# Two chained model blocks on one core: the order of VectorE's scalings and low halves in the norm between the blocks, and the PSUM banks around it

## The chip, the cores and the metric

The kernel runs on 1 core of one Trainium2 chip. The metric is the device time of one execution in microseconds (us), median of several. An engine is named as follows: TensorE (PE in the profile, PEld its weight loads), VectorE (DVE), ScalarE (ACT), GpSimd (POOL), SyncE (SP). All instruction streams run in order on their engine; semaphores tie them together.

## The reference

Two transformer blocks of different kind work on x, 512 tokens by 1024 channels in float32. The first mixes pooled averages and three-branch sparse attention and has a squared-ReLU feed-forward part; it ends with a norm. The second has a forgetting attention and a stick-breaking attention, 8 heads each, and 16 experts, of which each token takes 2. Where the one hands over to the other stands this:

```python
    x = x + jnp.square(jax.nn.relu(h @ w_ff1[l])) @ w_ff2[l]
    return rms_norm(x, norm_final)                      # end of the first block
...
    h = rmsnorm(x, norm1_g[l]) * (1.0 + scale1) + shift1    # start of the second
    proj = h @ w_in[l]
    qa, ka, va, fa, qb, kb, vb, ga, gb = jnp.split(proj, IN_SPLITS_2, axis=-1)
    log_f = jax.nn.log_sigmoid((fa + b_forget[l]).astype(jnp.float32)).transpose(0, 2, 1)
```

scale1 and shift1 come from a small product of the input c with ada_w. So the change stands between two norms in a row: that of norm_final, whose result is x from there on, and that of norm1_g.

## The kernel before, in words

All activations are held transposed: channels on the 128 partitions, the 512 tokens along the free axis, so x is eight row blocks X[:, k, :] of 128 by 512. A dense product is made in float32 precision from three passes in the fast format: each operand is split into a high half (ScalarE, a copy that rounds) and a low half (the difference). For weights the high half is L286 on ScalarE and the low half L291, in this part of the program on GpSimd. A weight tile of 128 by 1024 is loaded by SyncE's queue into one of five raw buffers and split into one of four split buffers. A written plan (make_plan) lists all weight tiles in order of use, and for each tile which later tile is loaded and which is split in its turn. `dense` (L417, L418, L421) is 24 matmuls of 128 by 512 for one output block; `dense_two` (L439, L440, L443) makes two output blocks at once and goes through the eight input blocks k in the outer loop, so that it can start when block 0 of the input is there: six matmuls for each k.

PSUM has eight banks. `Psum.take` gives the next matmul group a bank from a set, in turn: each set has its own counter. If the bank's last holder has not been read out, TensorE waits for the eviction before the group's first matmul. RB is the set of banks 0 to 6, ALL8 all eight. Bank 7 is otherwise kept for attention outputs and for the modulation's sums.

The norm between the blocks goes like this. ScalarE squares the row blocks, plain and times norm_final, VectorE and GpSimd add the squares up, and TensorE sums each over the partitions: `row_sums`, keys ("rms", 3) and ("rms", 4). ScalarE and VectorE make the two factors for each token from these, `diagonal` puts them into a diagonal matrix, and `spread` has TensorE spread them over the partitions: ("rmsb", 3) is the factor of norm_final, ("rmsb", 4) that of both norms together. Then for each row block k

- VectorE scales: TMP[k % 4] = X[k] * gsc * ps["rmsb", 4] (L1910),
- ScalarE adds shift1 and rounds: RH[0, k] (L1207),
- VectorE makes the low half: RH[1, k] = TMP + shift1 - RH[0, k] (L1913),

and TensorE, which waits for the low half of k, takes this block into dense_two with the tiles ("w2_fa", 0), the forget gates, and ("w2_qa", 0), the first of four for the queries. Behind the loop VectorE applies norm_final to the eight blocks of X in place (L1916).

The VectorE loop as it was, with the three instructions in this order for each k:

```python
            dve.scalar_tensor_tensor(TMP[:, j, :], X[:, k, :], gsc[:, 16 + k:17 + k], ps["rmsb", 4], ALU.mult,
...
            dve.wait_ge(*A(("h2", k)))
            dve.scalar_tensor_tensor(RH[:, 1, k, :], TMP[:, j, :], modt[:, k:k + 1], hif(RH[:, 0, k, :]), ALU.add,
```

What each engine has next. TensorE: dense products for ("w2_qa", 1), ("w2_qa", 2), ("w2_qa", 3), ("w2_ka", 0), ("w2_ka", 1) and then the first attention scores (`pair_scores(0)`, L753 and L758). ScalarE: the high half of a weight tile, ("w2_qa", 2); then the log-sigmoid chain for the forget gates, which starts by evicting ("w2_fa", 0) at L984 and goes on with an absolute value, exponential and logarithm (L1251 to L1255, with two loads of activation tables); then the high half of ("w2_qa", 3), and only then the eviction of ("w2_qa", 0) into PC, at L984 too, which stands in the same helper; then the high half of ("w2_ka", 0), the eviction of ("w2_qa", 1), and so on in turn. GpSimd: low halves of the same tiles. VectorE: the updates of X, then its part of the chain, which ends in a running sum along the tokens. SyncE: stores that sum to HBM, loads it back as rows spread over all partitions (L2551, four rows of 256 KB at first), which VectorE adds to the first scores (L1934), and loads the coming weight tiles.

Later follow the second attention's remaining parts, the output product, a third norm with the router, and the expert stage: for each unit of 128 token rows twelve weight tiles are loaded (w_gate, w_up, w_down), split by ScalarE (L286) and VectorE (L291), and used by TensorE.

Of the kernel before, what the change touches and what calls it, by code (L numbers as in the profile page):

```python
# [12 lines left out]
ALU = mybir.AluOpType  # L13
# [89 lines left out]
def hif(ap):  # L103
    return ap.bitcast(F32)
# [54 lines left out]
def build_program(nc, t, ctx):  # L159
    def sb(name, shape, dt=F32):  # L160
        return ctx.enter_context(nc.sbuf_tensor(name, shape, dt))

    def mark(name, step=1):
        m = Mark(ctx.enter_context(nc.semaphore(name)), step)
        marks.append(m)
        return m
# [3 lines left out]
    RH = sb("RH", [128, 2, 8, S], F32R)  # L170
# [4 lines left out]
    X = sb("X", [128, 8, S])  # L175
# [6 lines left out]
    TMP = sb("TMP", [128, 4, S])  # L182
# [10 lines left out]
    modt = sb("modt", [128, 48])  # L193
    gsc = sb("gsc", [128, 32])
# [9 lines left out]
    ps = Psum([ctx.enter_context(nc.psum_tensor(f"ps{i}", [128, 512], F32))[:, :] for i in range(8)])  # L204
# [4 lines left out]
    A = mark("act_done")  # L209
    LOV = mark("dve_weights_lo")  # L210
    V = mark("dve_done")
# [30 lines left out]
    for n, (name, u, kind) in enumerate(plan):  # L242
# [3 lines left out]
        if kind == "split":  # L246
            k = len(spl)
# [26 lines left out]
    def lo(n):  # L274

        return LOV(n) if lo_by[n] == "dve" else LOP(n)
# [31 lines left out]
    RST, GTS = RT[:, 0:512], RT[:, 512:704]  # L308
    NR = small[:, 32:56]
    SQ2 = PB[:, 0, 0:512]  # L310
# [45 lines left out]
    RB = (0, 1, 2, 3, 4, 5, 6)  # L356
# [37 lines left out]
    def tensor(pe):  # L394
        ps.restart()

        def take(key, banks=ALL8):
            b = ps.take(key, banks)
            if ps.prev[key] is not None:
                pe.wait_ge(*freed(ps.prev[key]))  # L400
            return b
# [25 lines left out]
        def dense_two(units, R, ready, banks=ALL8):  # L427

            tiles_ = [IDX[u] for u in units]
            bs = [take(u, banks) for u in units]  # L430
            for k in range(8):
                pe.wait_ge(*ready(k))
                for key, n, b in zip(units, tiles_, bs):
                    s, c = spl[n], 128 * k
                    wh, wl = RS[:, s, 0, c:c + 128], RS[:, s, 1, c:c + 128]
                    xh, xl = R[:, 0, k, :], R[:, 1, k, :]
                    if k == 0:
                        pe.wait_ge(*HI(n))
                    pe.matmul(b[:, :], wh, xh, start=(k == 0), stop=False)  # L439
                    pe.matmul(b[:, :], wh, xl, start=False, stop=False)  # L440
                    if k == 0:
                        pe.wait_ge(*lo(n))
                    last = pe.matmul(b[:, :], wl, xh, start=False, stop=(k == 7))  # L443
                    if k == 7:
                        last.then_inc(*P.up(key, ("fed", n)))
# [30 lines left out]
        def row_sums(key, acc, banks=ALL8):  # L476
            b = take(key, banks)
            for i in range(4):
                last = pe.matmul(b[:, i:i + 1], acc[:, 128 * i:128 * i + 128], onesf[:, 0:1], start=True, stop=True)
            last.then_inc(*P.up(key))  # L480

        def spread(key, j, banks=ALL8):
            b = take(key, banks)
            pe.wait_ge(*V(("dg", key)))
            pe.matmul(b[:, :], onesf[:, :], TMP[:, j, :], start=True, stop=True).then_inc(*P.up(key))
# [247 lines left out]


        pe.wait_ge(*V(("sq3", 7)))
        row_sums(("rms", 3), RST)
        pe.wait_ge(*V(("sq4", 7)))
        row_sums(("rms", 4), SQ2)
        spread(("rmsb", 4), 3, (4,))
        spread(("rmsb", 3), 2, (5,))  # L740


        def pair_scores(n):
# [49 lines left out]
        def projected(name, *us):  # L793
            for u in us:
                dense(name, u, RH, 0, 8, None, RB)

        dense_two([("w2_fa", 0), ("w2_qa", 0)], RH, lambda k: V(("h2", k)), (0, 1))
        projected("w2_qa", 1, 2, 3)
        projected("w2_ka", 0, 1)
        pair_scores(0)  # L800
# [651 lines left out]
    def vector(dve):  # L1452
        def tt(out, a, b, op, *keys):
            dve.tensor_tensor(out, a, b, op).then_inc(*V.up(*keys))  # L1454

        def after(*keys):

            for k in keys:
                dve.wait_ge(*V(k))
# [5 lines left out]
        def diagonal(key, col, j):  # L1465

            dg = TMP[:, j, :].rearrange("p (i n) -> p i n", i=4)
            tt(dg, identf[:, :].unsqueeze(1).broadcast_to([128, 4, 128]),
               NR[:, col:col + 4].unsqueeze(2).broadcast_to([128, 4, 128]), ALU.mult, ("dg", key))
# [223 lines left out]
        for n in range(18):  # L1693
# [14 lines left out]
            if n >= 3 and n % 2 == 1:  # L1708
                k = n // 2 - 1
# [188 lines left out]
        after("n2c")  # L1898
        diagonal(("rmsb", 4), 4, 3)
        diagonal(("rmsb", 3), 0, 2)  # L1900
        for k in range(8):
            j = k % 4
            if k == 0:
                dve.wait_ge(*P(("rmsb", 4)))
                after("ggs")
            elif k == 2:
                dve.wait_ge(*P(("rmsb", 3)))
            elif k >= 4:
                dve.wait_ge(*A(("h2", k - 4)))
            dve.scalar_tensor_tensor(TMP[:, j, :], X[:, k, :], gsc[:, 16 + k:17 + k], ps["rmsb", 4], ALU.mult,  # L1910
                                     ALU.mult).then_inc(*V.up(("h2w", k), ("ev", ("rmsb", 4))))
            dve.wait_ge(*A(("h2", k)))
            dve.scalar_tensor_tensor(RH[:, 1, k, :], TMP[:, j, :], modt[:, k:k + 1], hif(RH[:, 0, k, :]), ALU.add,  # L1913
                                     ALU.subtract).then_inc(*V.up(("h2", k)))
        for k in range(8):
            dve.scalar_tensor_tensor(X[:, k, :], X[:, k, :], GM_VECS(VG_FIN, k), ps["rmsb", 3], ALU.mult,  # L1916
                                     ALU.mult).then_inc(*V.up(("x2", k), ("ev", ("rmsb", 3))))
# [569 lines left out]
    def sync(sp):  # L2487
# [109 lines left out]
        sp.wait_ge(*OUT("all"))  # L2597

    engines = ((tensor, "tensor"), (scalar, "scalar"), (vector, "vector"), (gpsimd, "gpsimd"), (sync, "sync"))
    for body, _ in engines:  # L2600
        body(Dry())
    for m in marks:
        m.counting, m.n = False, 0
    block = ctx.enter_context(nc.Block())
    block.sync(sync)
    block.tensor(tensor)
    block.scalar(scalar)
    block.vector(vector)
    block.gpsimd(gpsimd)

# [140 lines left out]
```

## Time and profile before

| | |
|---|---|
| median of 3 runs | 1658.87 us (1653.78 to 1660.69) |
| the profiled execution | 1657.32 us |
| its span | 1655.5 us |
| TensorE busy | 1544.0 us, 93% of the span |
| VectorE busy | 894.5 us, 54% |
| ScalarE busy | 742.1 us, 45% |
| GpSimd busy | 679.8 us, 41% |
| mean granted TensorE clock | 0.976 of full speed |

The span is the time from the first to the last instruction of the profiled execution; its own time includes what lies around it. Busy time of TensorE counts overlapping matmuls once; where TensorE is the bound, only its idle time and stretches at a lower clock can be won. [...] A start-to-start distance in the timeline says how fast instructions follow each other; the duration of one can be longer, as they overlap.

### The profile page before, as it was taken

What the parts mean: (1) busy time and instruction counts of PE and PEld (TensorE: products, weight loads), DVE (VectorE), ACT (ScalarE), POOL (GpSimd) and SP (SyncE); (2) the same over time, 40 slices, a digit from 0 to 9 for tenths busy, and PEclk for the clock granted to TensorE, in tenths of its full rate; (3) what the DMA queues carried; (4) which work ended last, traced back from release to release, by engine and by line L of the source; (5) the groups of instructions that cost most, each with busy time, mean ns of one, the idle gap of its engine ahead of it and who ended that gap; (6) DMA issues with size and microseconds to landing.
All of it is one profiled execution on the core that took longest, in us unless ns stands there. A gap on an engine that the chain in (4) does not pass through costs nothing.

```text
span 1655.5 us, 19634 instructions
## 1 busy us (share of the span) xinstructions
PE 1544.0 (93%) x7371; PEld 1205.5 (73%) x7371; DVE 894.5 (54%) x1448; ACT 742.1 (45%) x1187; POOL 679.8 (41%) x421
## 2 busy tenths in 40 slices
PE   7988899999999999999986999999998899999982
PEld 6664566888887888888874777768886777777762
DVE  5357886143144665748325232441024689999984
ACT  5225786223243223232343544532233477777762
POOL 3244566444574646464552644735563200000003
PEclk9998999999999999999998999999998999999996
DMA  6420000422236584856321421112343799999944
GB/s 243 141 86 14 1 1 14 147 89 94 97 115 216 211 294 182 295 188 231 114 77 35 144 78 64 64 52 89 102 168 130 281 348 385 385 382 383 386 168 167
DMA packets 78542, 275.66 MB, mean 167 GB/s; under 512 B 9508, under 2 KB 10836, under 8 KB 78440
## 3 DMA queue, kind: packets, MB, share of 16 engines
q1 hardware_dynamic: 69712, 245.89, 41.6%
q10 hardware_dynamic: 6424, 20.05, 3.1%
q0 software_dynamic: 2304, 8.39, 1.4%
q8 instruction: 61, 1.00, 0.3%
q14 instruction: 41, 0.34, 0.1%
HBM read 243.84 MB, written 30.45 MB: 166 GB/s over the span
## 4 chain that ended last, share of the span: by engine, by line
PE 76%; DVE 10%; ACT 5%; issue 3%; POOL 2%; DMA 1%; PEldq 0%; SPq 0%; ACTq 0%; DVEq 0%; POOLq 0%
PE ps L417 16%; PE ps L421 16%; PE ps L418 16%; PE ps L922 2%; ACT RS L286 2%; PE ps L918 2%; PE ps L919 2%; PE ps L439 2%; DVE RS L291 2%; PE ps L443 2%; PE ps L440 2%; POOL RS L291 1%; PE ps L945 1%; PE ps L949 1%; PE ps L630 1%
## 5 line engine op out<-in xcount | busy, mean ns | idle before, releaser
L291 POOL TENSOR_TENSOR RS<-RAW,RS 128x1024 fp32r<-128x1024 f32 x174 | 433.2, 2492 | 448.8 <-ACT RS L286 448.6
L286 ACT ACTIVATE RS<-RAW 128x1024 fp32r<-128x1024 f32 x306 | 318.2, 1054 | 257.3 <-PE ps L421 147.4
L417 PE MATMUL ps<-RH,RS 128*128 128x512 f32 x816 | 325.3, 399 | 16.2 <-ACT RS L286 8.4
L421 PE MATMUL ps<-RH,RS 128*128 128x512 f32 x816 | 320.4, 393 | 1.2 <-POOL RS L291 1.2
L418 PE MATMUL ps<-RH,RS 128*128 128x512 f32 x816 | 320.3, 392 | 0.0
L417 PEld LDWEIGHTS ps<-RH,RS 128*128 128x128 f32 x816 | 154.8, 190 | 52.0 <-ACT RS L286 16.8
L421 PEld LDWEIGHTS ps<-RH,RS 128*128 128x128 f32 x816 | 154.7, 190 | 35.4 <-POOL RS L291 2.0
L418 PEld LDWEIGHTS ps<-RH,RS 128*128 128x128 f32 x816 | 154.9, 190 | 33.1 <-issue 1.4
L291 DVE TENSOR_TENSOR RS<-RAW,RS 128x1024 fp32r<-128x1024 f32 x132 | 154.8, 1220 | 24.1 <-ACT RS L286 23.6
L417 PE MATMUL ps<-RA,RS 128*128 128x512 f32 x400 | 157.5, 394 | 0.0
L418 PE MATMUL ps<-RA,RS 128*128 128x512 f32 x400 | 156.2, 390 | 0.0
L421 PE MATMUL ps<-RA,RS 128*128 128x512 f32 x400 | 156.1, 390 | 0.0
L2478 POOL DMA_INDIRECT PC<-ys,POS x2 | 1.9, 968 | 320.0 <-PEq L388 319.7
L922 PE MATMUL ps<-RS,RH 128*128 128x512 f32 x256 | 101.4, 396 | 7.4 <-DVE RS L291 7.4
L918 PE MATMUL ps<-RS,RH 128*128 128x512 f32 x256 | 102.7, 401 | 4.6 <-ACT RS L286 4.6
L1454 DVE TENSOR_TENSOR TMP<-TMP,ps 128x512 f32<-128x512 f32 x48 | 32.7, 685 | 128.1 <-ACT TMP L1172 72.4
L919 PE MATMUL ps<-RS,RH 128*128 128x512 f32 x256 | 99.8, 390 | 0.0
L417 PEld LDWEIGHTS ps<-RA,RS 128*128 128x128 f32 x400 | 75.4, 188 | 18.5 <-issue 3.0
L418 PEld LDWEIGHTS ps<-RA,RS 128*128 128x128 f32 x400 | 75.5, 189 | 15.9 <-issue 0.4
L421 PEld LDWEIGHTS ps<-RA,RS 128*128 128x128 f32 x400 | 75.4, 189 | 15.8
L1454 DVE TENSOR_TENSOR TMP<-ps,RT 128x512 f32<-128x512 f32 (+1 forms) x43 | 29.4, 686 | 73.1 <-PE ps L421 50.0
L922 PEld LDWEIGHTS ps<-RS,RH 128*128 128x128 f32 x256 | 48.0, 188 | 23.2 <-DVE RS L291 13.5
(357 smaller groups left out, 2633.6 us busy)
## 6 DMA issues: line engine op xcount, KB each, us to landing
RAW<-in_w_ff SPq DMA_DIRECT2D x64, 512.0 KB, 5.1
RAW<-in_w_gate SPq DMA_DIRECT2D x46, 512.0 KB, 6.3
RAW<-in_w_up SPq DMA_DIRECT2D x45, 512.0 KB, 7.2
RAW<-in_w_down SPq DMA_DIRECT2D x39, 512.0 KB, 6.0
PB<-in_ada SPq DMA_DIRECT2D x24, 512.0 KB, 4.3
TB<-in_ada SPq DMA_DIRECT2D x24, 512.0 KB, 4.4
xs<-TB SPq DMA_DIRECT2D x23, 512.0 KB, 8.6
M<-in_w_down SPq DMA_DIRECT2D x17, 512.0 KB, 6.0
```

The source lines that it names most:

```text
L286: act.activation(RS[:, spl[n], 0, :], raws[slot[n]], ACT.Copy).then_inc(*HI.up(n))
L291: eng.tensor_tensor(RS[:, s, 1, :], raws[slot[n]], hif(RS[:, s, 0, :]), ALU.subtract).then_inc(*mark.up(n))
L417: pe.matmul(b[:, :], wh, xh, start=(k == 0), stop=False)
L418: pe.matmul(b[:, :], wh, xl, start=False, stop=False)
L421: last = pe.matmul(b[:, :], wl, xh, start=False, stop=(k == K - 1))
L439: pe.matmul(b[:, :], wh, xh, start=(k == 0), stop=False)
L440: pe.matmul(b[:, :], wh, xl, start=False, stop=False)
L443: last = pe.matmul(b[:, :], wl, xh, start=False, stop=(k == 7))
L918: pe.matmul(b[:, :], xh, wh, start=(k == 0), stop=False)
L919: pe.matmul(b[:, :], xlo, wh, start=False, stop=False)
L922: last = pe.matmul(b[:, :], xh, wl, start=False, stop=(k == 7))
L1454: dve.tensor_tensor(out, a, b, op).then_inc(*V.up(*keys))
```

## The change

On VectorE, the scaling of block k + 1 is put ahead of the low half of block k. The scaling into TMP slot k % 4 waits for the low half of block k - 4 instead of for ScalarE's copy of it. On TensorE, the two sums of squares, the factor ("rmsb", 4) and the two tiles of dense_two take their banks in turn from RB; the factor ("rmsb", 3) goes to bank 7.

```diff
--- before.py
+++ after.py
@@ -733,11 +733,11 @@
 
 
         pe.wait_ge(*V(("sq3", 7)))
-        row_sums(("rms", 3), RST)
+        row_sums(("rms", 3), RST, RB)
         pe.wait_ge(*V(("sq4", 7)))
-        row_sums(("rms", 4), SQ2)
-        spread(("rmsb", 4), 3, (4,))
-        spread(("rmsb", 3), 2, (5,))
+        row_sums(("rms", 4), SQ2, RB)
+        spread(("rmsb", 4), 3, RB)
+        spread(("rmsb", 3), 2, (7,))
 
 
         def pair_scores(n):
@@ -794,7 +794,7 @@
             for u in us:
                 dense(name, u, RH, 0, 8, None, RB)
 
-        dense_two([("w2_fa", 0), ("w2_qa", 0)], RH, lambda k: V(("h2", k)), (0, 1))
+        dense_two([("w2_fa", 0), ("w2_qa", 0)], RH, lambda k: V(("h2", k)), RB)
         projected("w2_qa", 1, 2, 3)
         projected("w2_ka", 0, 1)
         pair_scores(0)
@@ -1898,20 +1898,24 @@
         after("n2c")
         diagonal(("rmsb", 4), 4, 3)
         diagonal(("rmsb", 3), 0, 2)
+        def h2_lo(k):
+            dve.wait_ge(*A(("h2", k)))
+            dve.scalar_tensor_tensor(RH[:, 1, k, :], TMP[:, k % 4, :], modt[:, k:k + 1], hif(RH[:, 0, k, :]), ALU.add,
+                                     ALU.subtract).then_inc(*V.up(("h2", k)))
+
         for k in range(8):
-            j = k % 4
             if k == 0:
                 dve.wait_ge(*P(("rmsb", 4)))
                 after("ggs")
             elif k == 2:
                 dve.wait_ge(*P(("rmsb", 3)))
             elif k >= 4:
-                dve.wait_ge(*A(("h2", k - 4)))
-            dve.scalar_tensor_tensor(TMP[:, j, :], X[:, k, :], gsc[:, 16 + k:17 + k], ps["rmsb", 4], ALU.mult,
+                after(("h2", k - 4))
+            dve.scalar_tensor_tensor(TMP[:, k % 4, :], X[:, k, :], gsc[:, 16 + k:17 + k], ps["rmsb", 4], ALU.mult,
                                      ALU.mult).then_inc(*V.up(("h2w", k), ("ev", ("rmsb", 4))))
-            dve.wait_ge(*A(("h2", k)))
-            dve.scalar_tensor_tensor(RH[:, 1, k, :], TMP[:, j, :], modt[:, k:k + 1], hif(RH[:, 0, k, :]), ALU.add,
-                                     ALU.subtract).then_inc(*V.up(("h2", k)))
+            if k >= 1:
+                h2_lo(k - 1)
+        h2_lo(7)
         for k in range(8):
             dve.scalar_tensor_tensor(X[:, k, :], X[:, k, :], GM_VECS(VG_FIN, k), ps["rmsb", 3], ALU.mult,
                                      ALU.mult).then_inc(*V.up(("x2", k), ("ev", ("rmsb", 3))))
```

How it moves instructions, first on VectorE. These are its first rows from the loop, before and after (L1910 became L1914, L1913 became L1903); the rows ahead of them are the same in both.

Before:

```order
733 L1910 SCALAR_TENSOR_TENSOR TMP<-X,gsc,ps 128x512 [waits dve_done,pe_done]
734 L1913 SCALAR_TENSOR_TENSOR RH<-TMP,modt,RH 128x512 [waits act_done]
735 L1910 SCALAR_TENSOR_TENSOR TMP<-X,gsc,ps 128x512
736 L1913 SCALAR_TENSOR_TENSOR RH<-TMP,modt,RH 128x512 [waits act_done]
737 L1910 SCALAR_TENSOR_TENSOR TMP<-X,gsc,ps 128x512 [waits pe_done]
738 L1913 SCALAR_TENSOR_TENSOR RH<-TMP,modt,RH 128x512 [waits act_done]
739 L1910 SCALAR_TENSOR_TENSOR TMP<-X,gsc,ps 128x512
740 L1913 SCALAR_TENSOR_TENSOR RH<-TMP,modt,RH 128x512 [waits act_done]
741 L1910 SCALAR_TENSOR_TENSOR TMP<-X,gsc,ps 128x512 [waits act_done]
742 L1913 SCALAR_TENSOR_TENSOR RH<-TMP,modt,RH 128x512 [waits act_done]
```

Here each scaling is followed by its own low half. After:

```order
733 L1914 SCALAR_TENSOR_TENSOR TMP<-X,gsc,ps 128x512 [waits dve_done,pe_done]
734 L1914 SCALAR_TENSOR_TENSOR TMP<-X,gsc,ps 128x512
735 L1903 SCALAR_TENSOR_TENSOR RH<-TMP,modt,RH 128x512 [waits act_done]
736 L1914 SCALAR_TENSOR_TENSOR TMP<-X,gsc,ps 128x512 [waits pe_done]
737 L1903 SCALAR_TENSOR_TENSOR RH<-TMP,modt,RH 128x512 [waits act_done]
738 L1914 SCALAR_TENSOR_TENSOR TMP<-X,gsc,ps 128x512
739 L1903 SCALAR_TENSOR_TENSOR RH<-TMP,modt,RH 128x512 [waits act_done]
740 L1914 SCALAR_TENSOR_TENSOR TMP<-X,gsc,ps 128x512 [waits dve_done]
741 L1903 SCALAR_TENSOR_TENSOR RH<-TMP,modt,RH 128x512 [waits act_done]
742 L1914 SCALAR_TENSOR_TENSOR TMP<-X,gsc,ps 128x512 [waits dve_done]
```

Two scalings stand at the beginning and, at the end, two low halves; between them they alternate as before, but each low half is one block behind. From the fifth scaling on the wait is for VectorE's own semaphore.

On TensorE the order is the same and only the banks differ (psN is bank N). Before and after, from the sums over the partitions (L479) and the factors (L485) to the first matmuls of dense_two (L439) and of the first dense tile behind it, ("w2_qa", 1) (L417):

```order
3333 L479 MATMUL ps7<-onesf,RT 128x1 [waits dve_done]
3334 L479 MATMUL ps7<-onesf,RT 128x1 x3
3335 L479 MATMUL ps0<-onesf,PB 128x1 [waits dve_done]
3336 L479 MATMUL ps0<-onesf,PB 128x1 x3
3337 L485 MATMUL ps4<-TMP,onesf 128x512 [waits dve_done]
3338 L485 MATMUL ps5<-TMP,onesf 128x512 [waits dve_done]
3339 L439 MATMUL ps1<-RH,RS 128x512 [waits dve_done,act_weights_hi]
3342 L439 MATMUL ps0<-RH,RS 128x512 [waits act_weights_hi]
3387 L417 MATMUL ps0<-RH,RS 128x512 [waits act_done,act_weights_hi]
3388 L418 MATMUL ps0<-RH,RS 128x512
3389 L421 MATMUL ps0<-RH,RS 128x512 [waits pool_weights_lo]
```

Banks 7, 0, 4 and 5 are taken by sums and factors, 1 and 0 by dense_two. After:

```order
3333 L479 MATMUL ps0<-onesf,RT 128x1 [waits dve_done]
3334 L479 MATMUL ps0<-onesf,RT 128x1 x3
3335 L479 MATMUL ps1<-onesf,PB 128x1 [waits dve_done]
3336 L479 MATMUL ps1<-onesf,PB 128x1 x3
3337 L485 MATMUL ps2<-TMP,onesf 128x512 [waits dve_done]
3338 L485 MATMUL ps7<-TMP,onesf 128x512 [waits dve_done]
3339 L439 MATMUL ps3<-RH,RS 128x512 [waits dve_done,act_weights_hi]
3342 L439 MATMUL ps4<-RH,RS 128x512 [waits act_weights_hi]
3387 L417 MATMUL ps5<-RH,RS 128x512 [waits dve_done,act_weights_hi]
3388 L418 MATMUL ps5<-RH,RS 128x512
3389 L421 MATMUL ps5<-RH,RS 128x512 [waits pool_weights_lo]
```

The first L417 goes to bank 0 before, the bank of ("w2_qa", 0), and waits for a ScalarE semaphore; after, it goes to bank 5, which ("w_ff2", 30) had last, and waits for one of VectorE. The tiles behind it follow in turn: ("w2_qa", 2) in bank 6, ("w2_qa", 3) in bank 0 and so on.

## Rows read from the trace of the kernel before

**Rows 1.** Waits, 850 to 915 us: waiter and releaser, us in total, times, longest.
```profile
PE ps L417 <- ACT PC L984: 6.3, 1, 6.3
PE ps L439 <- DVE RH L1913: 4.5, 8, 0.9
PEld ps L417 <- ACT RS L286: 6.7, 1, 6.7
```

**Rows 2.** Busy time by stretch: the norm, and TensorE's restart.
```profile
877.00:894.00 17.00, 12.93 (x48) 8.39 (x48) 11.46 (x18) 6.31 (x9) 1.17 (x1) 0.99 0.00 1
901.00:905.00 4.00, 4.00 (x11) 3.08 (x11) 2.48 (x1) 0.39 (x1) 4.00 (x2) 0.55 0.04 6
```

**Rows 3.** Timeline of VectorE: start us, us, engine, line, operation [idle before, releaser].
```profile
874.90 0.75 DVE L1910 SCALAR_TENSOR_TENSOR TMP<-X,gsc,ps 128x512 f32<-128x512 f32 x1 [1.63 <-PE ps L485]
876.43 0.75 DVE L1913 SCALAR_TENSOR_TENSOR RH<-TMP,modt,RH 128x512 fp32r<-128x512 f32 x1 [0.79 <-ACT RH L1207]
877.10 0.74 DVE L1910 SCALAR_TENSOR_TENSOR TMP<-X,gsc,ps 128x512 f32<-128x512 f32 x1
...
891.84 0.75 DVE L1913 SCALAR_TENSOR_TENSOR RH<-TMP,modt,RH 128x512 fp32r<-128x512 f32 x1 [0.79 <-ACT RH L1207]
892.50 5.35 DVE L1916 SCALAR_TENSOR_TENSOR X<-X,vecs,ps 128x512 f32<-128x512 f32 x8
```

**Rows 4.** Timeline of ScalarE: first copy, and the chain behind the norm.
```profile
875.68 0.72 ACT L1207 ACTIVATE RH<-TMP,modt 128x512 fp32r<-128x512 f32 x1 [4.14 <-DVE TMP L1910]
...
893.70 0.68 ACT L984 ACTIVATE TMP<-ps,vecs 8x512 f32<-8x512 f32 x1 [0.95 <-PE ps L443]
...
898.92 1.04 ACT L286 ACTIVATE RS<-RAW 128x1024 fp32r<-128x1024 f32 x1
899.87 0.57 ACT L984 ACTIVATE PC<-ps 128x512 f32<-128x512 f32 x1
```

**Rows 5.** Timeline of TensorE.
```profile
877.44 0.47 PE L439 MATMUL ps<-RH,RS 128*128 128x512 f32 x1 [0.88 <-DVE RH L1913]
877.75 0.40 PE L440 MATMUL ps<-RH,RS 128*128 128x512 f32 x1
877.98 0.40 PE L443 MATMUL ps<-RH,RS 128*128 128x512 f32 x1
...
892.64 0.50 PE L439 MATMUL ps<-RH,RS 128*128 128x512 f32 x1 [0.55 <-DVE RH L1913]
...
900.58 0.76 PE L417 MATMUL ps<-RH,RS 128*128 128x512 f32 x1 [6.29 <-ACT PC L984]
...
904.82 0.39 PE L418 MATMUL ps<-RH,RS 128*128 128x512 f32 x1
```

**Rows 6.** Timeline of GpSimd: low halves of dense weight tiles.
```profile
864.42 2.34 POOL L291 TENSOR_TENSOR RS<-RAW,RS 128x1024 fp32r<-128x1024 f32 x1 [1.78 <-ACT RS L286]
892.83 2.39 POOL L291 TENSOR_TENSOR RS<-RAW,RS 128x1024 fp32r<-128x1024 f32 x1 [26.06 <-ACT RS L286]
900.04 5.62 POOL L291 TENSOR_TENSOR RS<-RAW,RS 128x1024 fp32r<-128x1024 f32 x2 [4.82 <-ACT RS L286]
```

**Rows 7.** Timelines of SyncE's queue and of VectorE: the forget rows.
```profile
904.98 1.75 SPq L2551 DMA_DIRECT2D TMP<-nf  x4
...
931.85 0.69 DVE L1934 CUSTOM_DVE_ANT_0 PB<-ps,TMP 128x512 f32<-128x512 f32 x1 [28.38 <-PE ps L758]
```

**Rows 8.** Expert stage: two stretches, its longest wait, two pieces of its chain.
```profile
1300.00:1400.00 100.00, 94.30 (x476) 77.52 (x476) 83.62 (x99) 71.55 (x82) 6.55 (x7) 1.00 0.95 355
1400.00:1500.00 100.00, 95.38 (x438) 75.79 (x436) 89.72 (x95) 72.13 (x82) 0.00 (x0) 1.00 1.00 387
...
ACT RS L286 <- DVE TB L1454: 42.4, 14, 3.0
...
1436.43 1.07 ACT RS L286
...
1455.56 1.07 ACT RS L286
```

## The prediction

> **What bounds the kernel now.** I read the shares of busy time first: TensorE is busy 93% of the span, so only stretches in which it waits or runs slowly can give time back. Next the waits of the stretch around the change [rows 1]: TensorE waits 4.5 us in eight pieces for the low halves of the normed row blocks (L1913), and once, for 6.3 us, for ScalarE's eviction at L984. A third row puts 6.7 us of the weight loads' idle time down to ScalarE's L286; I come back to it. Then the rows by stretch [rows 2]; their columns are length, busy time (and count) of TensorE's matmuls, weight loads, VectorE, ScalarE and GpSimd, then granted clock. TensorE is busy 12.93 of 17 us in the norm; from 901 to 905, behind the hole, it is busy all the time, but at a granted clock of 0.55. Three losses, then, all beside this change: the stuttering loop, the hole, and the slow restart.
>
> The engines' own rows show the loop's recurrence. VectorE scales block k (L1910, 0.75 us), ScalarE makes the high half (L1207, 0.72), VectorE the low half (L1913, 0.75), and only behind that scales block k+1 [rows 3, 4]. Low halves begin at 876.43 and 891.84: seven periods of 2.20 us. TensorE has six matmuls for each block. They start 0.23 us apart (877.75, 877.98), the first after a wait 0.31 [rows 5], so six need 1.39 us without a wait. Its last group begins at 892.64.
>
> **Part 1, scaling ahead.** Nothing is added but the waits on VectorE's own low half of four blocks earlier, which has long ended when they are reached. The number of instructions is the same. With the clock of this stretch starting at the first scaling, 874.90: scaling of block 0 at 0; scaling of block 1 at 0.67, while ScalarE copies block 0 (0.78 to 1.50); low half 0 at 1.53, exactly where it is now. VectorE's starts stand 0.67 us apart (876.43 to 877.10), and the eight updates of X give (5.35 - 0.74) / 7 = 0.66 [rows 3]. So scaling and low half come every 1.34 us: low half 1 at 2.87, low half 6 at 9.57. ScalarE, 0.72 us for each block, is never behind, except at the end: scaling 7 starts at 8.90, its copy ends 1.50 later, low half 7 starts at 10.43, that is at 885.33 instead of 891.84. VectorE's 1.34 is shorter than TensorE's 1.39, so TensorE becomes the bound of the loop. Block 0 at 877.44 as now; its six matmuls take 0.08 more because of the first gap; block 1 at 878.91, then seven groups of 1.39 follow and the last ends its issue at 877.44 + 0.08 + 8 x 1.39 = 888.64. The last group's start moves from 892.64 to 887.25: **5.4 us**.
>
> [...]
>
> **Part 2, the banks.** Before, the first dense tile behind the loop (w2_qa, 1) takes PSUM bank 0, which (w2_qa, 0) has just filled. Its eviction is on ScalarE behind the forget-gate chain: bias (893.70), two table loads, exponential, logarithm, and a weight copy (898.92), then the eviction at 899.87 [rows 4]. TensorE starts at 900.58 [rows 5]. After, the tile takes bank 5, last used two tiles before the norm. Its weights must be there too. ScalarE and GpSimd split one tile ahead of each of the last feed-forward tiles; counted through the plan, the split of 864.42 [rows 6] is that of (w2_qa, 1), so both halves lie there since 866.8. The hole closes: start at 888.64 instead of 900.58, 11.94 us, of which 5.4 are part 1's and **6.5** the bank's.
>
> The granted clock was half in the hole's wake: ten steps from 900.58 to 904.82, 4.24 us, 0.42 each, against 0.23 [rows 5]. The hole gone, TensorE has no reason to drop: in the loop, with pauses of half a microsecond, it held 0.99 [rows 2]. Ten steps at 0.227 take 2.27: **2.0 us**.
>
> **What is late next.** TensorE moves by 13.9 us, the forget chain only by part 1's: it starts when (w2_fa, 0) is complete, 5.5 us earlier (888.2). So four things lose 8.4 us of slack. (w2_qa, 2): copied behind the last ScalarE copy, at about 885.3; low half done 888.7 (now 892.83 + 2.39 [rows 6]); wanted at 894.1. (w2_qa, 3): copy at 893.4 (now 898.92), low half done about 896.9; wanted at 899.5. This is the narrowest margin, 2.6 us. (w2_ka, 0): low half is the second of the pair of 5.62 us [rows 6], done 900.2, wanted 905.0. The forget rows from HBM: issued at 904.98 now, 899.5 then; first used by VectorE at 931.85 behind TensorE's scores, 917.9 then [rows 7]. 18 us is enough for four rows of 256 KB. So I cost all four at nothing. Beyond them TensorE is busy nearly without a break until the second norm, and what it waits for there is released by its own results, so the rest moves as a block. The sums' and factors' new banks add no wait: all were evicted before the last feed-forward tile was. The update of X still holds its bank until about 891.4, but that is bank 7 now, which the first attention output takes much later.
>
> **The sum.** 5.4 + 6.5 + 2.0 = 13.9 us. The profiled execution took 1657.32 us (span 1655.50), the median of the runs shown is 1658.87, 1.55 higher. 1657.32 - 13.9 = 1643.4 against the profiled one; on the median's footing 1645.0. Bounds of the unknown pieces: nobody has seen VectorE scale and make low halves alternately without a wait. If it were 0.75 from start to start instead of 0.67, TensorE would restart its group after a short wait each time, 8 x 0.1 = 0.8 us less gain. On the other side the loop can't beat TensorE's own 1.39, so no more than some tenths are to be had. The runs shown spread by 5 us below and 2 above their median, and this is the larger part of the range. A change under 0.5% (8.3 us) can't be told from none here.
>
> **Rivals.**
>
> *The bank is not what holds the tile.* The row of 6.7 us blames the copy of weights at L286, not the eviction [rows 1]. If the wanted weights were those of 898.92, the new bank would give nothing: TensorE would follow the chain, 5.5 us earlier, and hole and slow restart would stay. Gain 5.5, time 1653.4. Against it: the count through the plan above, and TensorE's start 0.14 us after the eviction's end (899.87 + 0.57), but 0.6 after the copy's. Chance 0.04.
>
> *The hole closes, and a smaller one opens.* Either the chain's weights come more than 2.6 us late for (w2_qa, 3), or TensorE is granted the full clock later. Before, the loop had room for that: six matmuls at 0.42 are 2.5 us, little over the period of 2.20. Now each group at half clock costs 2.5 - 1.4 = 1.1 us outright. Three groups: 3.4 us, time 1648.4. For it: ahead of 877.44 TensorE has only sums and factors to compute, the first 0.23 us step is that from 877.75 [rows 5], and one execution shows one moment only. Chance 0.10 for the two. [...]
>
> *Slower: the expert stage becomes bound by its transfers.* There, 14 units repeat every 19.13 us (1436.43 to 1455.56), the DMA engines are busy 1.00 of the time and move 387 GB/s [rows 8]. 19.13 us at 387 is 7.4 MB, and a unit's twelve weight tiles and two passages of rows, 512 KB each, are 7.3 MB: there is no reserve. The stretch before shows 355 GB/s. If the transfers fell to that in their new rhythm with TensorE, a unit would take 20.85 us, 14 units 24 us more: 1669. It decides from the point at which ScalarE's copies wait for a landing instead of for TensorE or VectorE. Against it: none of the stage's waits is for a DMA, the largest is ScalarE's for VectorE [rows 8], and the first loads are released by TensorE's own results, so they move with it. Chance 0.04.
>
> *The forecast*, 1645.0, has the remaining 0.82, with its own spread of 1640 to 1650.
>
> **How the numbers follow.** Leaving out the ends of 1653.4 and 1669 (0.08 together) and the tails of the others, the range of eight in ten is 1640 to 1651. Faster by over 0.5% means under 1650.6: nearly all of the forecast's case and most of the small hole's, 0.87. Within 0.5%: the bank rival and the rest, 0.09. Slower: 0.04.
>
> **What would show it.** Right: low halves 1.34 to 1.5 us apart; the L439 wait down from 4.5 us to under 1; the first L417 behind the loop at about 888.6, directly behind the last L443, with no wait for L984 and 0.23 us steps; the span up to the experts shorter by 14 us and the expert stage's period unchanged. Wrong: a wait of TensorE for L286 or GpSimd's L291 near 894 to 900, steps of 0.42 in the loop, or a unit's period over 19.2.

## The result, and the profile after

| | median of the runs | profiled execution | its span |
|---|---|---|---|
| before | 1658.43 us (1653.78 to 1660.69, 4 runs) | 1657.32 us | 1655.5 us |
| after | 1645.06 us (1644.81 to 1646.03, 4 runs) | 1646.03 us | 1644.2 us |

The ratio of the runs is 0.9924, 95% interval 0.9902 to 0.9946: 12.6 us less by the ratio, 13.4 by the medians. Forecast were 13.9 us and a median of 1645.0.

The waits of the stretch around the norm. Of [rows 1], L439's 4.5 us in eight pieces are 0.9 in one, and L417's 6.3 us for the eviction and the 6.7 us of weight loads are gone; ScalarE now waits for TensorE ahead of the chain:

```profile
ACT TMP L984 <- PE ps L443: 3.5, 1, 3.5
PE ps L439 <- DVE RH L1903: 0.9, 1, 0.9
```

VectorE, answering to [rows 3] (L1910 is L1914 now, L1913 is L1903). Two scalings, then alternation at 0.65 to 0.67 us from start to start, so 1.32 us for a block instead of 2.20; the last low half ends at 891.25 (889.62 + 1.63), 11.1 us behind the start of the first scaling, where it took 17.7:

```profile
880.15 1.41 DVE L1914 SCALAR_TENSOR_TENSOR TMP<-X,gsc,ps 128x512 f32<-128x512 f32 x2 [1.63 <-PE ps L485]
881.69 0.75 DVE L1903 SCALAR_TENSOR_TENSOR RH<-TMP,modt,RH 128x512 fp32r<-128x512 f32 x1
882.36 0.74 DVE L1914 SCALAR_TENSOR_TENSOR TMP<-X,gsc,ps 128x512 f32<-128x512 f32 x1
883.01 0.75 DVE L1903 SCALAR_TENSOR_TENSOR RH<-TMP,modt,RH 128x512 fp32r<-128x512 f32 x1
...
889.62 1.63 DVE L1903 SCALAR_TENSOR_TENSOR RH<-TMP,modt,RH 128x512 fp32r<-128x512 f32 x2
```

ScalarE's chain, answering to [rows 4]. It is as long as before; (w2_qa, 0) is still evicted only behind it, at 901.14, but nobody waits for that:

```profile
894.96 0.68 ACT L984 ACTIVATE TMP<-ps,vecs 8x512 f32<-8x512 f32 x1 [3.54 <-PE ps L443]
...
901.14 0.57 ACT L984 ACTIVATE PC<-ps 128x512 f32<-128x512 f32 x1
```

TensorE, answering to [rows 5]. From 882.69 the 48 matmuls of the loop and the 24 of (w2_qa, 1) follow each other with no gap; L417 begins at 895.38, 0.23 behind the last L443. New is the half clock at the loop's start: eight slow steps from 882.69 to 886.24, the first of 0.56 us (0.31 in the kernel before) and seven of 0.43.

```profile
872.62 1.87 PE L479 MATMUL ps<-onesf,RT 128*128 128x1 f32 x8 [5.21 <-DVE RT L1454]
...
882.69 0.77 PE L439 MATMUL ps<-RH,RS 128*128 128x512 f32 x1 [0.87 <-DVE RH L1903]
883.25 0.63 PE L440 MATMUL ps<-RH,RS 128*128 128x512 f32 x1
...
886.24 0.41 PE L443 MATMUL ps<-RH,RS 128*128 128x512 f32 x1
886.49 0.40 PE L439 MATMUL ps<-RH,RS 128*128 128x512 f32 x1
...
895.15 0.39 PE L443 MATMUL ps<-RH,RS 128*128 128x512 f32 x1
895.38 0.39 PE L417 MATMUL ps<-RH,RS 128*128 128x512 f32 x1
```

GpSimd, answering to [rows 6], in two rows. The first low half of the group that begins at 901.31 is that of (w2_qa, 3); TensorE, 48 steps of 0.227 behind 895.38, needs it for a third matmul at 906.7:

```profile
891.49 2.40 POOL L291 TENSOR_TENSOR RS<-RAW,RS 128x1024 fp32r<-128x1024 f32 x1 [19.48 <-ACT RS L286]
901.31 8.03 POOL L291 TENSOR_TENSOR RS<-RAW,RS 128x1024 fp32r<-128x1024 f32 x3 [7.42 <-ACT RS L286]
```

Busy time by stretch, columns as in [rows 2], clock third from the end. The clock is 0.50 in the loop's first four us, 0.97 in the next, and 1.00 where the hole was. In the last row, the expert stage has the pace of before [rows 8]:

```profile
882.00:886.00 4.00, 3.31 (x8) 2.69 (x9) 4.00 (x7) 1.98 (x4) 0.00 (x0) 0.50 0.02 4
886.00:890.00 4.00, 4.00 (x19) 3.23 (x18) 4.00 (x7) 2.21 (x4) 0.00 (x0) 0.97 0.00 0
894.00:901.00 7.00, 7.00 (x32) 5.81 (x31) 3.45 (x6) 5.95 (x7) 0.00 (x0) 1.00 0.00 0
1400.00:1500.00 100.00, 95.72 (x441) 76.50 (x440) 91.29 (x96) 74.56 (x85) 0.00 (x0) 1.00 0.99 382
```

**Where the 11.3 us between the two spans are.** I cut both executions at four marks: the start of the sums (L479), the first L417 behind the loop, the first router matmul (L861) and the first gather of GpSimd behind the experts.

| stretch | before | after | difference |
|---|---|---|---|
| start to sums | 867.37 | 872.62 | +5.25 |
| sums to first L417 | 33.21 | 22.76 | -10.45 |
| first L417 to router | 377.19 | 375.36 | -1.83 |
| router to gather | 350.30 | 346.19 | -4.11 |
| gather to end | 27.43 | 27.27 | -0.16 |

The change accounts for the second and third line, 12.3 us. The first and fourth belong to no edit. They go with the granted clock, as two stretches of the first attention and one of the last expert unit show; before:

```profile
120.00:140.00 20.00, 15.03 (x46) 9.58 (x47) 12.50 (x31) 6.51 (x19) 11.13 (x10) 0.74 0.15 53
180.00:200.00 20.00, 17.54 (x121) 10.94 (x122) 17.41 (x61) 15.45 (x46) 10.83 (x12) 1.00 0.01 2
1612.00:1616.00 4.00, 3.99 (x10) 3.14 (x11) 1.23 (x1) 1.06 (x1) 0.00 (x0) 0.50 0.32 131
```

And after, with the last expert product at its own place in time:

```profile
120.00:140.00 20.00, 15.81 (x47) 9.79 (x48) 12.54 (x32) 6.67 (x19) 11.29 (x10) 0.66 0.15 52
180.00:200.00 20.00, 17.36 (x102) 10.28 (x104) 15.42 (x54) 13.92 (x42) 9.52 (x10) 0.84 0.00 1
1604.00:1608.00 4.00, 3.70 (x16) 3.10 (x17) 1.43 (x2) 1.06 (x1) 0.00 (x0) 1.00 0.35 131
```

From 180 to 200 us TensorE ran at 0.84 instead of 1.00. The whole of the first line arises around there: the same ScalarE instructions start 0.3 us earlier in the execution after than in the one before at 142.9 us, but 1.6 us later at 168.2, 3.8 at 193.3 and 5.3 at 218.3, and it stays at 5.3 from there to the sums. That the clock is what delays them is read from the two profiles; no experiment shows it. In the last unit, whose product follows a wait of 2.9 us in both executions, it was the other way round: 13 steps at half clock before, none after, which is 2.8 of the fourth line's 4.1 us. The other 1.3 us lie in pieces ahead of this product and behind it, and were not traced. The two lines nearly cancel here, and don't in other executions.

### The profile page after: what moved, and what is told of

It is laid out like the page before. It is cut to its first block, busy times and chain, and to the rows that moved or that the text cites. A ratio compares the mean times of both kernels' runs of the same rounds, so it can differ in the third digit from the quotient of the medians.

```text
span 1644.2 us, 19634 instructions
## 1 busy us (share of the span) xinstructions
PE 1544.7 (94%) x7371; PEld 1206.5 (73%) x7371; DVE 893.7 (54%) x1448; ACT 742.8 (45%) x1187; POOL 680.2 (41%) x421
## 4 chain that ended last, share of the span: by engine, by line
PE 77%; DVE 10%; ACT 5%; issue 3%; POOL 2%; DMA 1%; SPq 0%; PEldq 0%; ACTq 0%; DVEq 0%; POOLq 0%
PE ps L417 16%; PE ps L421 16%; PE ps L418 15%; PE ps L922 2%; ACT RS L286 2%; PE ps L918 2%; PE ps L919 2%; PE ps L439 2%; PE ps L440 2%; PE ps L443 2%; PE ps L630 2%; DVE RS L291 2%; POOL RS L291 1%; PE ps L949 1%; PE ps L945 1%
## 5 line engine op out<-in xcount | busy, mean ns | idle before, releaser
L286 ACT ACTIVATE RS<-RAW 128x1024 fp32r<-128x1024 f32 x306 | 318.2, 1054 | 259.0 <-PE ps L421 147.4
L417 PE MATMUL ps<-RH,RS 128*128 128x512 f32 x816 | 323.8, 397 | 10.3 <-ACT RS L286 8.7
L417 PEld LDWEIGHTS ps<-RH,RS 128*128 128x128 f32 x816 | 154.0, 189 | 45.2 <-ACT RS L286 10.5
L417 PE MATMUL ps<-RA,RS 128*128 128x512 f32 x400 | 157.2, 393 | 0.0
L417 PEld LDWEIGHTS ps<-RA,RS 128*128 128x128 f32 x400 | 75.5, 189 | 18.6 <-issue 3.0
```

The lines of the kernel that those rows point to most:

```text
L286: act.activation(RS[:, spl[n], 0, :], raws[slot[n]], ACT.Copy).then_inc(*HI.up(n))
```

## The experiments

Each was timed in alternation with the kernel before on the same chip. "Sums to L417" is the second line of the table above, from the run's own profile.

| run | median, us | before there | ratio (95%) | sums to L417 | half-clock steps in the loop |
|---|---|---|---|---|---|
| e1_order | 1653.66 (12) | 1658.67 (22) | 0.9969 (0.9956 to 0.9982) | 29.27 | 8 |
| e2_banks | 1651.33 (11) | 1658.67 (22) | 0.9952 (0.9935 to 0.9969) | 26.77 | 7 |
| e3_two_banks | 1644.59 (6) | 1658.67 (22) | 0.9917 (0.9898 to 0.9936) | 22.65 | 7 |
| e4_warm | 1644.31 (6) | 1658.67 (22) | 0.9907 (0.9885 to 0.9929) | 19.81 | 0 |
| e5_after_late | 1647.60 (6) | 1662.10 (17) | 0.9913 (0.9893 to 0.9933) | 22.79 | 8 |
| e6_before_late | 1665.03 (12) | 1662.10 (17) | 1.0021 (1.0004 to 1.0037) | 37.83 | 8 |
| e7_two_ahead | 1647.37 (4) | 1662.10 (17) | 0.9913 (0.9890 to 0.9936) | 21.89 | 0 |
| e8_warm_more | 1650.88 (6) | 1662.10 (17) | 0.9935 (0.9918 to 0.9953) | 19.82 | 0 |
| a1_again | 1647.43 (6) | 1658.75 (10) | 0.9925 (0.9898 to 0.9951) | 22.75 | 8 |
| e9_warm_third | 1641.42 (5) | 1658.75 (10) | 0.9898 (0.9879 to 0.9916) | 19.81 | 0 |

### The order alone

```diff
-        row_sums(("rms", 3), RST, RB)
+        row_sums(("rms", 3), RST)
...
-        spread(("rmsb", 3), 2, (7,))
+        spread(("rmsb", 3), 2, (5,))
...
-        dense_two([("w2_fa", 0), ("w2_qa", 0)], RH, lambda k: V(("h2", k)), RB)
+        dense_two([("w2_fa", 0), ("w2_qa", 0)], RH, lambda k: V(("h2", k)), (0, 1))
```

> VectorE's order of the change with the banks of before. Theory (loop 5.4, bank 6.5, restart 2.0 us): the loop runs at TensorE's pace, but (w2_qa, 1) still takes bank 0 and waits for the eviction behind the forget-gate chain, which starts some 5 us earlier. Hole of some 6.3 us and half-clock restart stay. 5.4 us less than before, about 1653.0. In the profile L417 waits for L984 some 6 us. Rival (the bank never held the tile, all of the gain is the order): as fast as the change, about 1645.

5.0 us less, forecast 5.4. TensorE's waits in the stretch:

```profile
PE ps L417 <- ACT PC L984: 6.3, 1, 6.3
...
PE ps L439 <- DVE RH L1903: 0.9, 1, 0.9
```

The loop's stutter is gone, the hole of 6.3 us is whole, and 11 half-clock steps follow it. The rival, that the order is all, is out.

### The banks alone

The reverse: the five bank arguments of the change in the kernel before.

> The banks of the change with VectorE's order of before. Theory: the loop keeps its period of 2.20 us, the hole and the half-clock restart go: 6.5 + 2.0 = 8.5 us less than before, about 1650.0. No wait of L417 for L984 behind the loop; the L439 waits of some 4.5 us stay. Rival (L417 waited for its weights): the time of before, 1658.4.

7.3 us less by the medians, 8.0 by the ratio, forecast 8.5. The hole is gone (33.21 to 26.77 us, 6.4). The two parts add up: 3.9 us for the order alone and 6.4 for the banks alone, 10.45 together in the change. TensorE at the loop's start and end:

```profile
880.35 0.77 PE L439 MATMUL ps<-RH,RS 128*128 128x512 f32 x1 [0.91 <-DVE RH L1913]
880.91 0.63 PE L440 MATMUL ps<-RH,RS 128*128 128x512 f32 x1
...
883.86 0.39 PE L443 MATMUL ps<-RH,RS 128*128 128x512 f32 x1
...
895.52 0.50 PE L439 MATMUL ps<-RH,RS 128*128 128x512 f32 x1 [0.55 <-DVE RH L1913]
...
896.79 0.39 PE L443 MATMUL ps<-RH,RS 128*128 128x512 f32 x1
897.01 0.39 PE L417 MATMUL ps<-RH,RS 128*128 128x512 f32 x1
```

This run also answers a question of the profile after. It has seven half-clock steps at the loop's start, the profiled kernel before has none, and yet the loop's last matmul starts at the same distance from the start of the sums (26.55 and 26.54 us): in this loop, with its period of 2.20 us, the half clock is hidden. In the new one it isn't.

### Which of the five banks counts

The change with sums and factors in their banks of before, and dense_two in (2, 3).

> The change, but sums and factors keep their banks of before (7, 0, 4, 5) and only the two tiles of the loop move, to banks 2 and 3. Theory: only the bank that the tile behind the loop needs counts, so this is as fast as the change, about 1645 (within 1.5 us). Rival (the banks of sums and factors matter too): slower by 1 us or more in the stretch from the sums to the first L417 behind the loop.

1644.59, and 22.65 us from the sums to L417 against 22.76. The banks of sums and factors are worth nothing that this stretch shows; it was the pair of the loop that stood on the next tile's bank.

### The chain made longer, after and before

```diff
         act.wait_ge(*A("fy"))
+        for i in range(7):
+            act.activation(TMP[0:8, 1, :], TMP[0:8, 0, :], ACT.Abs).then_inc(*A.up(("late", i)))
+            act.wait_ge(*A(("late", i)))
```

> The change, with seven more absolute values (0.63 us each, 0.66 with its wait) in ScalarE's forget-gate chain, so that all behind it comes 4.6 us later. Theory: the chain is off TensorE's path now, with 2.6 us of room (low half of (w2_qa, 3) ready 2.6 us before TensorE wants it). So TensorE waits 2.0 us ahead of (w2_qa, 3), and the time is 2 us more than the change's: about 1647. Rival A (the room is larger than counted): no difference. Rival B (something else behind the chain, the forget rows or the next weight loads, is nearer to the edge): the whole 4.6 us or more, about 1650.

> The kernel before with the same seven operations. Theory: there the chain holds (w2_qa, 0)'s bank and with it TensorE, so all 4.6 us count: the hole of 6.3 us becomes 10.9, about 1663.3. Rival (the hole belongs to weights or to something else that is not behind the chain): the time of before.

TensorE's waits, of the change with the longer chain and then of the kernel before with it:

```profile
PE ps L421 <- POOL RS L291: 1.5, 1, 1.5
```

```profile
PE ps L417 <- ACT PC L984: 10.9, 1, 10.9
```

Before, the hole grows from 6.3 to 10.9 us, all of the 4.6 added. In the timing this is 0.0021 more, 3.5 us, with an interval (0.7 to 6.1 us) that holds 4.6. After, TensorE waits 1.5 us, for the low half of (w2_qa, 3): the next thing late is the one that was named, with 3.1 us of room instead of 2.6, since the low half is needed only for the tile's third matmul, 0.46 us behind the first. The timing of the whole kernel does not resolve 1.5 us; the wait row does.

### Two blocks ahead

```diff
-            if k >= 1:
-                h2_lo(k - 1)
+            if k >= 2:
+                h2_lo(k - 2)
+        h2_lo(6)
         h2_lo(7)
```

> The change, with VectorE scaling two blocks ahead of the low half instead of one. Theory: the loop is TensorE's already (0.23 us steps against VectorE's 1.32 us for a block), so the last L439 group does not start earlier; block 0's low half comes up to 0.5 us later, since two scalings go ahead of it: the same time, 1645, or 0.5 us more. Rival (VectorE's recurrence still sets the pace): 1 us or more less.

VectorE's first three groups:

```profile
879.43 1.41 DVE L1914 SCALAR_TENSOR_TENSOR TMP<-X,gsc,ps 128x512 f32<-128x512 f32 x2 [1.63 <-PE ps L485]
881.14 0.75 DVE L1914 SCALAR_TENSOR_TENSOR TMP<-X,gsc,ps 128x512 f32<-128x512 f32 x1 [0.30 <-PE ps L485]
881.80 0.74 DVE L1903 SCALAR_TENSOR_TENSOR RH<-TMP,modt,RH 128x512 fp32r<-128x512 f32 x1
```

The third scaling waits 0.30 us for the second factor's matmul (the wait at k = 2), and the loop starts 10.91 us behind the start of the sums instead of 10.07, 0.84 later than in the change, where up to 0.5 was forecast. In this execution the clock had risen before the loop; 48 matmuls took 10.98 us, 0.229 each. The loop is TensorE's, and going further ahead costs 0.8 us at its start. A timing of four runs, 0.9913, can't tell it from the change.

### The clock held up

```diff
+        def warm(b, n):
+            for _ in range(n):
+                pe.matmul(b[:, :], RA[:, 0, 0, 0:128], RA[:, 0, 0, :], start=True, stop=True)
```

> The change, with 29 matmuls of no use on TensorE ahead of the sums (20), ahead of the first factor (6) and ahead of the loop (3), written into the bank that the next useful matmul overwrites. In the profile of the change TensorE computed sums, factors and the loop's first 8 matmuls at half clock. Theory: with the added work the granted clock stays at full level through sums, factors and loop; every L439 step is 0.23 us, the factor matmuls 0.6 instead of 1.06 us each pass, so 1.6 us from the loop and 1 to 2 us from sums and factors: about 1642 (1641 to 1643.5). Rival (the added matmuls stand in the way of the sums and factors, or the clock does not follow): 1645 or more.

TensorE between the last feed-forward tile and the loop (L479 is the added work here; sums are L487, factors L494, the loop L440 to L444):

```profile
867.52 4.70 PE L479 MATMUL ps<-RA 128*128 128x512 f32 x20
872.97 1.05 PE L487 MATMUL ps<-onesf,RT 128*128 128x1 f32 x8 [0.75 <-DVE RT L1462]
874.45 1.05 PE L487 MATMUL ps<-onesf,PB 128*128 128x1 f32 x8 [0.43 <-DVE PB L1462]
875.36 2.00 PE L479 MATMUL ps<-RA 128*128 128x512 f32 x6
877.28 3.25 PE L494 MATMUL ps<-TMP,onesf 128*128 128x512 f32 x4
879.97 1.25 PE L479 MATMUL ps<-RA 128*128 128x512 f32 x3
881.74 0.50 PE L440 MATMUL ps<-RH,RS 128*128 128x512 f32 x1 [0.52 <-DVE RH L1911]
```

Sums to L417 fall from 22.76 to 19.81 us, 2.95: 1.6 in the loop, 1.3 ahead of it. The forecast's step held for the sums and the loop, not for the factors: the clock fell behind the sums all the same and rose again just ahead of the loop, as two stretches show (clock third from the end):

```profile
876.00:878.00 2.00, 2.00 (x6) 1.05 (x5) 1.64 (x4) 0.10 (x1) 0.00 (x0) 0.61 0.00 0
878.00:880.00 2.00, 2.00 (x5) 0.74 (x3) 0.60 (x1) 0.00 (x0) 0.00 (x0) 0.54 0.00 0
```

The forecast time did not quite come: 1644.31 against 1642, six runs in two heaps (1639.92 to 1641.45, and 1647.18 to 1647.83). The profiled execution is of the upper heap, and its sums begin at 872.97, late by the clock of the first attention. So the total says little at six runs: its interval overlaps the change's. The partner runs below say more.

> The kernel with the added matmuls around the norm (e4_warm), and 46 more in four holes of TensorE in the first attention (16, 10, 8 and 12 of them), in which the granted clock fell in some profiled executions and not in others (0.66 to 1.00 by stretch between 120 and 200 us; the sums of this norm begin at 867.4 in the execution with the clock high and at 870 to 873 in the others). Theory: those holes are where the 5 us of spread between executions comes from; filled, the sums begin at 868 or earlier in every execution, and the time is some 4 us under e4_warm's median, 1640, with less spread. Rival (the clock falls anyway, or the added work delays the next product): 1644 or more.

This went wrong: 1650.88 us against 1640 forecast, and a ratio worse than e4_warm's. It went wrong by the same rule as the hole. `take` waits for the bank's last holder, and I put the added work behind it. Three rows of TensorE, of the first, a later and the second place:

```profile
118.97 3.92 PE L499 MATMUL ps<-RH 128*128 128x512 f32 x16
...
129.65 2.70 PE L610 MATMUL ps<-M,X 64*128 64x384 f32 x10 [3.56 <-DVE TMP L1505]
...
148.35 2.57 PE L499 MATMUL ps<-RH 128*128 128x512 f32 x10 [2.58 <-DVE stat L1639]
```

At 118.97 the work fills the gap and the clock of 120 to 140 rises from 0.66 to 0.83, but TensorE then waits 3.56 us for VectorE at 129.65: this stage is VectorE's. At 148.35 the added matmuls themselves wait 2.58 us for the bank and then stand 2.4 us in the way. The sums begin at 877.35, 4.4 us later than in e4_warm. So the theory that the spread comes from those holes is not tested by it; it stays open.

> The changed kernel again, unchanged, as the partner of the next one on the same chip. By the first result 0.9924 of before, 13 to 14 us less. Its loop, being TensorE's now, should again take 1.5 to 1.6 us more than 11.1 when the clock rises inside it, and none when it rises ahead of it.

> e4_warm (added matmuls around the norm between the blocks), and 20 more in the third norm, ahead of its sums (9), factor (6) and router product (5), where the profile of the change shows TensorE waiting 2.2, 1.4 and 1.7 us and running at half clock behind (0.86 over 1250 to 1300). Theory: 2.9 us from the norm between the blocks, as e4_warm's profile shows, and 1 to 2 us from the router product's 16 matmuls (1061 ns each at half clock): 4 us less than the changed kernel of this job. Rival (what is won there is lost to the clock elsewhere, or the router product follows ScalarE and VectorE, not TensorE): less than 2 us.

On one chip, 1647.43 for the change again (1639.07 to 1651.24) and 1641.42 with 29 and 20 added matmuls (1638.31 to 1644.68). TensorE in the third norm:

```profile
1254.67 2.20 PE L479 MATMUL ps<-RH 128*128 128x512 f32 x9
1257.07 1.05 PE L487 MATMUL ps<-onesf,RT 128*128 128x1 f32 x8 [0.20 <-DVE RT L1462]
1257.99 1.64 PE L479 MATMUL ps<-RH 128*128 128x512 f32 x6
1259.46 1.08 PE L494 MATMUL ps<-TMP,onesf 128*128 128x512 f32 x2
1259.98 1.71 PE L479 MATMUL ps<-RH 128*128 128x512 f32 x5
1262.23 5.56 PE L869 MATMUL ps<-M,VBK 128*32 128x512 f32 x16 [0.54 <-ACT M L1374]
```

From the first L417 to the router 374.14 us against 375.24, so 1.1 us there, from sums and factor, and 2.94 from the norm between the blocks: 4.0 us in places where the edit acts, the amount forecast. The rest of the 6 us between the medians falls in no stretch that the edit touches. But the 1 to 2 us that were forecast from the router product did not come: it took 5.56 us against 5.61, though its matmuls now ran at full clock, 0.59 to 0.62 us each instead of 1.06. Both before and now its pairs of matmuls follow ScalarE's eight blocks, which come 0.66 us apart, so this piece of the rival was right. The ratios, 0.9898 (0.9879 to 0.9916) and 0.9925 (0.9898 to 0.9951), overlap, so the timing alone does not place this version ahead of the change; the 2.95 us from sums to L417 are there in all three profiles with the added work. By its median it is the fastest of all.

## Why the prediction was right, point by point

**The loop, 5.4 us.** Right in mechanism and close in size. VectorE: 1.34 us for a block forecast, 1.32 measured; the last low half at 10.43 after the first scaling, measured 10.35 (890.50, its end less the 0.75 of one, against 880.15). TensorE became the bound, as said. The order alone gave 5.0 us by the medians (3.0 to 7.3 by the ratio's interval), and in its profile 3.9 from sums to L417, since TensorE paid the half clock inside the loop.

**The bank, 6.5 us.** Right: 33.21 to 26.77 in e2_banks, and the hole's length follows the chain one to one (e6_before_late). The rival that took the row of 6.7 us at its word (weights, L286) is refuted by both. The row is idle time of the weight loads. It names the copy that ended at 899.96, though the eviction ended later, at 900.44, and the first load began at 900.55; with the other bank, in e2_banks, TensorE goes on with no wait for any copy.

**The slow restart, 2.0 us.** Right: first L417 to router is 1.83 us shorter.

**The sum, 13.9 us, and 1645.0.** The medians moved 13.4, and the stretches of the change 12.3. The term that was missed is the clock in the loop, and one of the prediction's own signs of being wrong, steps of 0.42 us in the loop, did appear. The clock was forecast as full from 877.44, because that one execution had it so; the 0.99 of [rows 2] starts just there and says nothing of where the rise falls in another execution. Of six profiles with the new order and no added work, four (the change twice, e1_order, e5_after_late) had eight half-clock steps in the loop, e3_two_banks seven and only e7_two_ahead none, at 0.2 us each: 1.4 to 1.6 us. This was priced as a rival at 1.1 us for each group of six, with 0.10 for it together with late weights; it happened for a group and a third, and should have been the likelier case. The exactness of the total owes something to chance: the four runs of before scatter by 6.9 us, the six of a1_again by 12.2, and there the medians are 11.3 us apart.

**What is late next.** None of the four was late: in the profile after, TensorE has no wait from 895 to 945 us. The narrowest slack, forecast as 2.6 us, measured 3.1 (e5_after_late); the other three were not measured. (w2_ka, 2), which I had not listed, shows in the profile after as a wait of ScalarE for a landing, 1.8 us, with no cost.

**The slower rival.** The expert unit takes 19.12 us (1433.29 to 1452.41) against 19.13, at 382 GB/s: nothing of it happened.

**Start to start on VectorE.** The durations of the pair add up to 1.49 us (0.74 and 0.75), and the pairs came every 1.32: in the loop of the profile after, each operation started 0.08 to 0.09 us before the recorded end of the one ahead of it.

**The rise of the clock.** It came at most 10.1 us after the start of the sums in one execution (before: 0.50 granted from 872 to 877 us, 1.00 from 877.4 to 879) and 13.6 us after it in others (after: 886.2 - 872.62; e2_banks: 883.9 - 870.24), 3.5 us apart. In all three TensorE waits between sums and factors and again ahead of the loop (before: 1.88 and 0.88 us).

## What to carry to other kernels

Where two products share few buffers that are evicted behind a long chain on another engine, the next product pays for the chain; give the pair the buffers that come free last, and look at the eviction's place in its engine's queue, not at its duration. A recurrence over three engines is cut by letting the first engine run one step ahead, and one is enough when the consumer becomes the bound. The half clock that the loop with its period of 2.20 us had hidden cost 1.4 to 1.6 us once TensorE was the loop's bound, in five of six profiles: price such steps where TensorE has been idle ahead of a stretch, or try to fill the idle time with matmuls, ahead of every wait, the buffer's own included. Here 29 of them shortened the stretch from sums to L417 by 2.95 us in three profiles, while the time of the whole kernel did not resolve it.

## What the runs showed of the hardware that I had not expected

The start of the sums, which no edit but e8_warm_more's touches, lay between 867.37 and 873.25 us in the other profiles. In the earliest three (867.37, 868.28, 868.42) the granted clock over 120 to 140 us was 0.74 and over 180 to 200 at least 0.94; in the five latest (872.61 to 873.25) it was 0.66 and 0.83 or 0.84. The change itself stands at both ends, 868.42 in a1_again and 872.62. So executions of one kernel differ by 4 to 5 us ahead of this mark, and the later they are, the lower the granted clock of one stage; that the clock is the cause was not tested. The last expert unit adds up to 2.8 us (13 steps at half clock). Why an execution takes the one way or the other is open.
